# Dealing a side computation's turns evenly over the blocks of two expert stages

## The reference

```python
def first_block(x, ...):
    for i in range(DEPTH):
        hn = rms_norm(h, norm_mix[i])
        h = h + (forgetting_attention(...) if i % 2 == 0 else retention(...))
        hn = rms_norm(h, norm_ffn[i])
        h = h + hier_moe(hn, ..., expert_w_gu[i], expert_w_down[i])   # 32 experts, all weights are read
...
def second_block(x, c, ctx, ...):
    xc = ctx
    for l in range(DEPTH):
        pc = (rmsnorm(xc, norm1_g[l]) * (1.0 + scc1) + shc1) @ w_in[l] + b_in[l]
        h_c, st_f, st_b = mlstm_bidir(qc, kc, vc, gtc, zs, zs, not last)
        ...                                                            # the same for x, from the context's states
        if not last:
            xc = xc + gc1 * (y_c @ w_out[l])
            xc = xc + gc2 * swiglu(rmsnorm(xc, norm2_g[l]) * (1.0 + scc2) + shc2, w_gu[l], w_down[l])
```

## Time and profile before

| | |
|---|---|
| median of 3 launches | 2326.18 us (2323.99 to 2330.57) |
| the profiled launch | 2321.29 us, of which the span from first to last instruction is 2319.4 us |
| TensorE clock granted, mean | 0.962 of full speed |
| PE, DVE, ACT busy in the span | 92%, 48%, 38% |
| expert stage 0 | about 230 to 735 us of the span |
| expert stage 1 | about 1001 to 1580 us of the span |

### The profile page before, as it was taken

The page is one execution under the profiler, slowest core; times in us unless marked ns, Lnnn a source line. Parts: engine busy times, 40 slices in busy tenths (PEclk is TensorE's granted clock), DMA queues, the critical chain, the costliest instruction groups (busy, mean ns, idle before and its releaser), DMA issues. The chain is left out here.

```text
span 2319.4 us, 44748 instructions
## 1 busy us (share of the span) xinstructions
PE 2134.2 (92%) x19290; PEld 1729.8 (75%) x19290; DVE 1118.5 (48%) x1956; ACT 872.1 (38%) x1474; POOL 84.0 (4%) x160
## 2 busy tenths in 40 slices
PE   7998988998886999989999999978989999988999
PEld 7957566765554987967777776646878998868999
DVE  6464435433513644543333334424865555765554
ACT  4444242242212443432222223334444444554443
POOL 0000000000000000000110110000000000000001
PEclk9999999999998999999999999999989999989999
DMA  8577999999998567699999999998426556514550
GB/s 297 164 254 283 393 425 420 379 380 426 425 421 361 194 227 287 226 386 410 399 382 400 417 411 369 367 408 325 161 79 255 183 169 206 192 55 141 182 177 29
DMA packets 128077, 676.22 MB, mean 292 GB/s; under 512 B 11488, under 2 KB 11744, under 8 KB 65920
## 3 DMA queue, kind: packets, MB, share of 16 engines
q1 hardware_dynamic: 111616, 614.77, 68.1%
q0 software_dynamic: 16256, 58.50, 6.6%
HBM read 672.17 MB, written 1.05 MB: 290 GB/s over the span
## 5 line engine op out<-in xcount | busy, mean ns | idle before, releaser
L496 PE MATMUL bank<-xx,high 128*128 128x256 f32 (+1 forms) x3296 | 624.0, 290 | 20.2 <-DVE xx L657 13.8
L496 PEld LDWEIGHTS bank<-xx,high 128*128 128x128 f32 (+1 forms) x3296 | 518.5, 193 | 68.3 <-issue 50.9
L496 PE MATMUL bank<-xx,low 128*128 128x256 f32 (+1 forms) x1648 | 471.2, 286 | 0.0
L496 PEld LDWEIGHTS bank<-xx,low 128*128 128x128 f32 (+1 forms) x1648 | 317.8, 193 | 0.9
L445 DVE TENSOR_TENSOR low<-lane,high 128x1024 fp32r<-128x1024 f32 (+1 forms) x112 | 130.7, 1170 | 258.2 <-ACT high L434 258.0
L434 ACT ACTIVATE high<-lane 128x1024 fp32r<-128x1024 f32 (+1 forms) x112 | 113.1, 1013 | 291.8 <-PE bank L496 288.7
L496 PE MATMUL bank<-hx,high 128*128 128x256 f32 x1056 | 197.1, 288 | 0.0
L496 PEld LDWEIGHTS bank<-hx,high 128*128 128x128 f32 x1056 | 164.1, 191 | 16.4 <-issue 15.7
L496 PE MATMUL bank<-hx,low 128*128 128x256 f32 x528 | 149.0, 282 | 0.0
L496 PE MATMUL bank<-gth,high 128*128 128x256 f32 x384 | 112.5, 293 | 6.6 <-DVE gtl L655 5.2
L1489 ACT ACTIVATE hs<-bank 64x256 f32<-64x256 f32 x64 | 24.2, 378 | 245.1 <-PE bank L1476 244.9
(11 more groups left out here) (607 smaller groups left out, 3997.3 us busy)
## 6 DMA issues: line engine op xcount, KB each, us to landing
ring__14<-in_expert_gu_blocks SPq DMA_DIRECT2D x36, 1024.0 KB, 10.8
ring__15<-in_expert_gu_blocks SPq DMA_DIRECT2D x35, 1024.0 KB, 10.2
ring__16<-in_expert_gu_blocks SPq DMA_DIRECT2D x35, 1024.0 KB, 9.8
lane<-in_w_gu_blocks POOLq DMA_DIRECT2D x44, 512.0 KB, 8.3
ring__48<-in_expert_gu_blocks SPq DMA_DIRECT2D x18, 1024.0 KB, 13.0
ring__160<-in_expert_gu_blocks SPq DMA_DIRECT2D x18, 1024.0 KB, 9.5
ring__161<-in_expert_gu_blocks SPq DMA_DIRECT2D x18, 1024.0 KB, 9.6
ring__159<-in_expert_gu_blocks SPq DMA_DIRECT2D x18, 1024.0 KB, 9.9
```

What stands on the lines that cost most here:

```text
L496: done = pe.matmul(out, a.bitcast(F32R), b.bitcast(F32R), start=it["start"] and k == 0 and q == 0 and not halves, stop=stop)
```

## The change

Only the dealing of turns changes. `dense` held a last block for each place (b < n); it holds now a range of blocks (b in n).

```diff
@@ schedule
-                        for _ in range((place in places) + any(place == z and b < n for z, n in dense)):
+                        for _ in range((place in places) + any(place == z and b in n for z, n in dense)):
                             next(turns, None)
@@ stage 0
-                              (("up", 1), ("up", 3), "across", ("down", 0)), ((("down", 1), 16),), NE - 2)
+                              (("up", 1), ("up", 3), "across", ("down", 0)), ((("down", 1), range(3, NE, 2)),), NE - 2)
@@ stage 1
-                              (("up", 0), ("up", 1), ("up", 2), ("up", 3), "across", ("down", 0)), ((("down", 1), NE), ("across", 12)), NE)
+                              (("up", 0), ("up", 1), ("up", 2), ("up", 3), "across", ("down", 0)), ((("down", 1), range(NE)), ("across", range(20, NE))), NE)
```

## The result

The changed kernel takes **2346.12 us** (median of 5 launches, 2339.09 to 2347.36) against 2326.49 us (5 launches, 2323.99 to 2332.0) for the kernel before on the same chip: ratio 1.0071, 95% interval 1.0055 to 1.0088. It is slower, by 20 us where 1 us faster was forecast, and outside the range. On another chip the ratio was 1.0061 (1.0046 to 1.0075).

What follows compares the result with a forecast made beforehand. PE was taken to set the pace until its last hold-up of the loads in each stage, the loads after it. Stage 0's -4.5 and stage 1's +3.5 gave -1.0 us from 2326.18: 2325 us, range 2315 to 2334.

Steps and rivals of the forecast that it cites:

- What bounds the kernel: Both expert stages: PE sets the pace up to its last hold-up of the loads, then the remaining bytes do.
- last hold-up: Last moment PE holds up the loads: block 16 in stage 0, near 504 us; block 27 in stage 1, near 1515.
- Stage 0, -4.5 us: Block 16: six light turns fewer, 5.4 us sooner, less about 1 us of PE waiting; deferred turns free; -4.5 us.
- rival 2: Stage 0 gains more: the stop at 398 to 422 us nearly vanishes, -10 there; 2317 us; chance 0.12.
- Stage 1, even dealing worth 0: Stage 1 up to block 27: PE's sum is unchanged by turns moved from blocks 4 to 11 to 20 on; 0 us.
- The second norm, +3.5 us: Stage 1, norm's new place in its block: +1.8 before the sums, +1.3 idle behind them, +0.4 clock; +3.5 us.
- The end of stage 1 stays with the loads: Blocks 28 to 32: loads set the pace; eight turns a block add at most 0.9 us more in a block.
- The clock, +0.4 us: Stage 1, second norm: a longer idle makes PE's already falling clock a little worse, +0.4 us.
- Rival 3: Second norm in its new position costs 9 us or more, stage 0 gains nothing: +9, 2335 us; chance 0.18.

Runs made afterwards that it cites:

- fastest run: Stage 0 dealt evenly as in the change; stage 1 dealt as before it, except four turns in block 26 and three in block 27: 2308.14 us, 0.9917 of before.
- stage 0 alone: Kernel before, with only stage 0 dealt evenly as in the change: 2318.31 us (0.9954 of before), and 2318.09 us (0.9959) when run again.
- the run with the steps in one go: Kernel before, no turn moved, all side steps (routing of extra blocks) issued at once after block 23: 2346.37 us, 1.0079 of before.
- The run with even dealing and old places: Stage 0 even as changed; stage 1's eight-turn blocks spread over blocks 4, 6, ... 20, turns from block 22 at their old places: 2321.80 us, 0.9976 of before.
- the steps begun later: Changed kernel, with the side steps begun after block 24 in place of block 23: 2335.29 us, 1.0031 of before.

## Why the prediction was wrong

**What bounds the kernel**, PE up to a last hold-up and then the loads, agrees with the runs as far as they test it. Twelve turns moved behind block 27 brought the mark of block 28 7.7 us sooner, and behind the last hold-up the loads get 425 to 426 GB/s (after: 426 from the mark of block 29 on; fastest run: 425 from that of block 28).

**Stage 0, -4.5 us** had the right mechanism and sign, and a size too small. The trace says -6.9, the launches of stage 0 alone -8.5 and -10.3. The stop near 400 us shrank (323 to 390 GB/s) and so did that before block 17 (376 to 420), as in rival 2. Up to block 17 PE was busy 242.05 us against 250.95, 8.9 less where the six turns were priced at 5.4; it was 9.3 us sooner there. The deferred turns, priced at nothing, were not quite free: in every trace with stage 0 even the way from block 17 to the last mark took 213.7 to 216.6 us, against 212.3 to 212.8 with stage 0 as before (the run with the steps in one go left aside).

**Stage 1, even dealing worth 0**: right up to block 22. Blocks 4 to 11 took 20.8 us each (forecast 20.0; 2.7 us of the difference is one wait at L470 behind the first norm, which I had not seen coming), blocks 20 to 22 took 20.7, and PE was full in both but for that wait (163.84 of 166.50 us). The run with even dealing and old places agrees to within 2 to 3 us.

**The second norm, +3.5 us** is the step that failed. The wait ahead of the sums came out at 0.89 us (forecast 2.8). The idle behind them came out at 18.2 (forecast 5.6). The sentence at fault is "and then the projection's high and low parts, some 1.3 us": I added durations along the chain as if DVE's queue held nothing else. Listed by DVE's own order, 25 side steps and the one-hot steps stand in that gap. With the side steps gone the idle is 8.8, of which 1.8 are the one-hot steps by their rows; the other 1.4 above the forecast no run takes apart. The Trainium skill (PSUM — Partial Sum Buffer, Engine vs sequencer instructions) says in plain words that VectorE's and ScalarE's queues are strict FIFO, and the rows agree. The prediction followed the order of the program on PE only.

**"The end of stage 1 stays with the loads"** failed as well, and it weighs more. The last hold-up moved from block 27 to block 28, where the split L2618 cost 3.7 us more in one wait. Of the 22.0 us by which stage 1 grew, 6.9 went with the side steps, 11.3 more with the last blocks dealt otherwise (six light turns fewer among them), and 3.8 were left. In PE's account of the 22.0 us: PE busy 539.34 against 535.27, so 4.1 are slower matmuls, and 17.9 are idle.

**The clock, +0.4 us**: 4.1 us of slower matmuls in stage 1, ten times the term and as large as what I gave stage 0. Over the whole span PE was busy 157 us at a granted clock of 0.50 before and 183 us after. As a pass takes up to twice as long there (L1530 1.93 us against 1.07), an estimate from these numbers is that the lower level costs at most some 80 us of the span before and 90 after, over 3%. The remark of the Trainium skill (TensorE: Matmul & The Clock Gate, Part 1), cited in the prediction, that the ramp is under 1% of a typical span is hard to square with that: even a third of it would be over 1%.

**Rival 3** named the right place (the norm, slower by over 9 us) with the wrong mechanism, and priced it without a look at DVE's queue; stage 0 did gain. That the sign of rival 3 came true, at twice its size, is thus in part luck.

## What to carry to other kernels

When a change moves work between places in a program, list for each engine, not only for the one that waits, what now stands ahead of each instruction that somebody waits for; generators that the diff does not name count too. Dealing side work is a question of order as well as of number: six turns moved gave stage 1 4.0 to 4.7 us, and the seventh, which brought the others back to their old places in the block, 2.8 more, three times its own price. And do not read a wait as time of the launch: 9.4 us of idle taken away gave 6.9 us of the stage.

## What the runs showed of the hardware

The longer idle did not bring the longer slow stretch behind it. In the changed kernel PE stood idle from 1439.1 us, the granted clock fell to 0.50 (1.2 of 2.4 GHz) at 1443.7, and it was full again 3.4 us after PE's restart. By stretch, columns as in the earlier trace rows, then the passes:

```profile
1457.30:1460.70 3.40, 3.38 (x29) 1.91 (x33) 2.76 (x6) 0.00 (x0) 1.05 (x2) 0.50 0.53 114
1460.80:1472.60 11.80, 11.80 (x138) 7.61 (x131) 3.64 (x5) 3.46 (x5) 1.06 (x2) 1.00 1.01 398
```

```profile
1457.62 2.09 PE L1557 MATMUL bank<-tmp,y 32*128 32x256 f32 x16
1459.64 1.58 PE L1530 MATMUL bank<-ring__15,ht 128*32 128x256 f32 x16
1461.15 0.41 PE L496 MATMUL bank<-xx,high 128*16 128x256 f32 x2
```

With the steps begun later PE stood idle from 1438.1 us, 8.77 us in place of 18.20; the clock fell at 1442.6 and was full again 5.9 us after the restart:

```profile
1446.90:1452.70 5.80, 5.80 (x41) 3.00 (x42) 0.01 (x1) 0.00 (x0) 1.05 (x2) 0.50 0.95 369
```

```profile
1447.18 2.09 PE L1557 MATMUL bank<-tmp,y 32*128 32x256 f32 x16
1449.20 1.94 PE L1530 MATMUL bank<-ring__15,ht 128*32 128x256 f32 x16
1451.06 0.61 PE L496 MATMUL bank<-xx,high 128*16 128x256 f32 x2
```

PE was busy 541.78 us in that stage 1 against 539.34. Of these 2.4 us, 1.15 lie in block 24 (16.43 us against 15.28), and 1.30 in block 25 (27.15 against 25.85), where the clock fell once more (mean 0.88 against 0.94). Taking a wait away can thus cost a part of its gain at the lower level of the clock: 9.4 us less idle shortened the stage by 6.9.
